# Last feed-forward stage of a two-block transformer step: three pairs of column chunks by seven block products instead of two, one weight sum of each on a DMA

## The reference

```python
h2 = rmsnorm_2(x, norm_mlp_g[l])
up = jnp.square(jax.nn.relu(jnp.einsum('bsd,df->bsf', h2, w_up[l])))   # w_up 1024 x 4096
x = x + jnp.einsum('bsf,fd->bsd', up, w_down[l])                       # w_down 4096 x 1024
```

## Time and profile before

| | us |
|---|---|
| median of 3 runs | 981.1 (980.86 to 981.48) |
| the profiled execution, its own time | 980.97 |
| its span, first to last instruction | 979.2 |
| TensorE busy | 970.4 (99%) |
| VectorE busy | 765.6 (78%) |
| ScalarE busy | 658.5 (67%) |
| GpSimd busy | 118.9 (12%) |

### The profile page before, as it was taken

The page is one execution under the profiler, slowest core; times in us unless marked ns, Lnnn a source line. Parts: engine busy times, 40 slices in busy tenths (PEclk is TensorE's granted clock), DMA queues, the critical chain, the costliest instruction groups (busy, mean ns, idle before and its releaser), DMA issues.

```text
span 979.2 us, 12257 instructions
## 1 busy us (share of the span) xinstructions
PE 970.4 (99%) x4528; PEld 796.2 (81%) x4528; DVE 765.6 (78%) x1010; ACT 658.5 (67%) x887; POOL 118.9 (12%) x109
## 2 busy tenths in 40 slices
PE   8999999999999999999999999999999999999998
PEld 7788888888777788888888788888888888888887
DVE  6798797668987666888797677777689878977675
ACT  7677576577666536766566586868875548877782
POOL 0000000022300000000000041159913001000000
DMA  8998937696444536986826586677666664695532
GB/s 263 314 313 276 278 117 234 198 322 193 134 152 146 172 129 215 274 254 212 267 67 224 167 249 227 168 177 204 205 214 215 234 196 151 211 319 170 191 111 94
DMA packets 167589, 202.12 MB, mean 206 GB/s; under 512 B 58081, under 2 KB 113770, under 8 KB 167402
## 3 DMA queue, kind: packets, MB, share of 16 engines
q1 hardware_dynamic: 166938, 201.21, 66.6%
q10 hardware_dynamic: 592, 0.14, 0.1%
HBM read 182.45 MB, written 5.77 MB: 192 GB/s over the span
## 4 chain that ended last, share of the span: by engine, by line
PE 92%; DVE 3%; DMA 2%; ACT 1%; issue 1%; POOL 1%; SPq 0%; ACTq 0%; DVEq 0%; POOLq 0%
PE bank L2650 22%; PE bank L2652 22%; PE bank L2651 22%; PE bank L2803 4%; PE bank L2805 4%; PE bank L2804 4%; PE bank L2923 3%; PE bank L2921 3%; PE bank L2922 3%; PE bank L2665 1%; DMA raw<-in_ffn_w_down 1%; PE bank L2957 1%; PE bank L3072 1%; DVE lo L1820 1%; DVE lo L1837 0%
## 5 line engine op out<-in xcount | busy, mean ns | idle before, releaser
L2650 PE MATMUL bank<-hi,xh 128*128 128x512 f32 (+1 forms) x824 | 328.0, 398 | 0.9 <-DVE lo L2251 0.7
L2652 PE MATMUL bank<-hi,xl 128*128 128x512 f32 (+1 forms) x824 | 320.6, 389 | 0.0
L2651 PE MATMUL bank<-lo,xh 128*128 128x512 f32 (+1 forms) x824 | 319.8, 388 | 0.0
L1820 DVE TENSOR_TENSOR lo<-raw,hi 128x2048 fp32r<-128x2048 f32 (+1 forms) x87 | 198.4, 2285 | 59.9 <-ACT hi L1114 59.7
L1114 ACT ACTIVATE hi<-raw 128x2048 fp32r<-128x2048 f32 (+1 forms) x90 | 170.8, 1902 | 86.9 <-PE bank L2652 37.1
L2650 PEld LDWEIGHTS bank<-hi,xh 128*128 128x128 f32 x824 | 154.8, 188 | 34.2 <-issue 1.7
L2652 PEld LDWEIGHTS bank<-hi,xl 128*128 128x128 f32 x824 | 154.7, 188 | 32.7
L2651 PEld LDWEIGHTS bank<-lo,xh 128*128 128x128 f32 x824 | 155.0, 188 | 29.8
L1837 DVE TENSOR_TENSOR lo<-raw,hi 128x1024 fp32r<-128x1024 f32 (+1 forms) x108 | 132.3, 1234 | 40.3 <-ACT hi L1123 39.5
L1123 ACT ACTIVATE hi<-raw 128x1024 fp32r<-128x1024 f32 x102 | 104.5, 1051 | 10.0 <-PE bank L2652 10.0
L2803 PE MATMUL bank<-hi,hh 128*128 128x512 f32 x176 | 69.2, 393 | 2.2 <-DVE hl L1946 2.2
(11 more groups left out here) (315 smaller groups left out, 1499.8 us busy)
## 6 DMA issues: line engine op xcount, KB each, us to landing
raw<-in_w_in SPq DMA_DIRECT2D x48, 1024.0 KB
raw<-in_ffn_w_gu SPq DMA_DIRECT2D x50, 512.0 KB
raw<-in_ffn_w_down SPq DMA_DIRECT2D x22, 1024.0 KB
first_operand<-in_ffn_w_gu SPq DMA_DIRECT2D x32, 512.0 KB
raw<-in_w_down SPq DMA_DIRECT2D x16, 1024.0 KB
raw<-in_w_out SPq DMA_DIRECT2D x8, 1024.0 KB
last_operand<-in_w_up SPq DMA_DIRECT2D x8, 1024.0 KB
raw<-in_w_up SPq DMA_DIRECT2D x8, 1024.0 KB
```

The source lines that it names most:

```text
L1820: nc.vector.tensor_tensor(lo[s][:, :, 0:width], whole(n)[:, :, 0:width], hi[s][:, :, 0:width].bitcast(F32), ALU.subtract).then_inc(lo_done, 1)
L2650: nc.tensor.matmul(o, sh, wh, start=first and j == 0, stop=False, skip_group_check=onto)
L2651: nc.tensor.matmul(o, sh, wl, start=False, stop=False, skip_group_check=onto)
L2652: ins = nc.tensor.matmul(o, sl, wh, start=False, stop=last and j == 3, skip_group_check=onto)
```

## The change

- `PAIRS = (2, 4, 6)`: chunks 4 and 5 become a pair, in the unit order of the other two; `plain_chunks` and `plain_up`'s waits for it go.
- In the last stage the fourth sum of each pair (operand 1 += operand 5) leaves VectorE and becomes a DMA with `accum_op=add` on GpSimd's queue, SBUF to SBUF, 1 MB. ScalarE's `split_hi` of p4 waits for it (`t4_in`), and so does the next pair's second sum, which overwrites operand 5. `SUMS_MADE` counts four sums per pair in the gated stages and three in the last.
- The other three sums of the next pair move into `pair_chunks` on VectorE: the first behind `add_product(j, 1)` and ahead of the split of p3, the second behind the split of p2 of the next pair and ahead of `last_lo(i)`, the third behind the split of p6.
- SyncE's order in the last stage is one loop over the pairs; the load of the next pair's block 3 now stands ahead of `flip_last(i, 1)`.
- Gated stages: `ffn_planes(f, i+1, ...)` moves ahead of `ffn_hi(f, i)` in `gated_pair`, and in the second pair `ffn_hi(f, 9)`, `ffn_merge(f, 9)` and `ffn_lo(f, 9)` move in front of, or between, the steps of chunk 10.

```diff
-PAIRS = (2, 6)
+PAIRS = (2, 4, 6)
...
@@ block_free
-                elif PAIR_AT[j][1] == PAIRS[1] or j in (1, 3):
+                elif j > LAST_PAIR:
+                    sp_eng.wait_ge(lo_done, pair_unit(j - 1, ("p1", "p4", "p7", "p3")[b]) + 1)
+                    if b == 0:
+                        sp_eng.wait_ge(pairs.t_made, SUMS_MADE[j - 1] + 1)
+                    elif b == 3:
+                        sp_eng.wait_ge(pairs.t_made, SUMS_MADE[j])
+                elif j in (1, 3):
...
@@ SyncE, last stage
+            for j in range(LAST_PAIR, len(PAIR_AT)):
+                i = PAIR_AT[j][1]
+                if i < NF2 - 2:
+                    last_block(j + 1, 0)
+                last_load("d", i - 1, 1)
+                last_load("d", i, 0)
+                flip_last(i, 0)
+                if i < NF2 - 2:
+                    last_block(j + 1, 2)
+                    last_block(j + 1, 1)
+                last_load("d", i, 1)
+                if i < NF2 - 2:
+                    last_block(j + 1, 3)
+                flip_last(i, 1)
+                last_load("d", i + 1, 0)
+                flip_last(i + 1, 1)
+                flip_last(i + 1, 0)
+            last_load("d", NF2 - 1, 1)
...
@@ GpSimd, at its end
+            def fourth_sum(j):
+
+                pool.wait_ge(pairs.t_made, SUMS_MADE[j] + 2)
+                pool.wait_ge(lo_done, pair_unit(j, "p2") + 1)
+                nc.gpsimd.dma_start(last_operand[1][:, :, :], last_operand[5][:, :, :],
+                                    accum_op=ALU.add).then_inc(pairs.t4_in, UNIT_IN)
...
@@ ScalarE gated_pair
+                ffn_planes(f, i + 1, 1)
+                ffn_planes(f, i + 1, 0)
                 ffn_hi(f, i)
                 split_hi(n + 12)
-                ffn_planes(f, i + 1, 1)
-                ffn_planes(f, i + 1, 0)
+                if j % 2 == 1:
+                    ffn_hi(f, i + 1)
                 ffn_act(f, i + 2, 0)
...
@@ VectorE gated_pair
                 split_lo(n + 12)
+                if j % 2 == 1:
+                    ffn_merge(f, i + 1)
                 ffn_hidden(f, i + 2, 0)
+                if j % 2 == 1:
+                    ffn_lo(f, i + 1)
                 ffn_hidden(f, i + 2, 1)
...
@@ VectorE pair_chunks, last stage (from the first pair's branch on)
-                    weight_sum(j, 4)
...
                     add_product(j, 0)
                     split_lo(unit_of("p6", i))
+                    weight_sum(j, 3)
                     split_lo(unit_of("d", i - 2, 1))
...
                 add_product(j, 1)
+                if more:
+                    weight_sum(j + 1, 1)
                 split_lo(unit_of("p3", i))
                 split_lo(unit_of("d", i - 1, 1))
                 last_merge(i)
                 add_product(j, 2)
                 split_lo(unit_of("d", i - 1, 1) + 1)
-                last_lo(i)
-                split_lo(unit_of("d", i - 1, 1) + 2)
+                if more:
+                    split_lo(unit_of("d", i - 1, 1) + 2)
+                    weight_sum(j + 1, 2)
+                    last_lo(i)
+                else:
+                    last_lo(i)
+                    split_lo(unit_of("d", i - 1, 1) + 2)
```

More of the change, by code:

```diff
@@ L128 @@
 LAST_PAIR = len(PAIR_AT) - len(PAIRS)
+SUMS_MADE = [4 * min(j, LAST_PAIR) + 3 * max(0, j - LAST_PAIR)
+             for j in range(len(PAIR_AT) + 1)]
 def unit_of(kind, i, b=0):
@@ L1107, in split_hi @@
                 elif KINDS[n] in OPERAND:
-                    act.wait_ge(pairs.t_made, 4 * pair_of(n) + {"p5": 1, "p6": 2, "p7": 3, "p4": 4}[KINDS[n]])
+                    j = pair_of(n)
+                    if KINDS[n] == "p4" and j >= LAST_PAIR:
+                        act.wait_ge(pairs.t4_in, UNIT_IN * (j - LAST_PAIR + 1))
+                    else:
+                        act.wait_ge(pairs.t_made, SUMS_MADE[j] + {"p5": 1, "p6": 2, "p7": 3, "p4": 4}[KINDS[n]])
                 else:
@@ L1449, in last_ffn @@
                 last_hi(0)
[L1450 to L1454, removed]
+                for j in range(LAST_PAIR, len(PAIR_AT)):
+                    pair_chunks(j)
                 split_hi(UNITS - 2)
@@ L1880, in weight_sum @@
                     dve.wait_ge(pairs.b_in[3], UNIT_IN * (j + 1))
+                    if j > LAST_PAIR:
+                        dve.wait_ge(pairs.t4_in, UNIT_IN * (j - LAST_PAIR))
                 elif t == 4:
@@ L1884, in weight_sum @@
                 if t > 1:
-                    dve.wait_ge(pairs.t_made, 4 * j + t - 1)
+                    dve.wait_ge(pairs.t_made, SUMS_MADE[j] + t - 1)
                 dst, left, right = ((4, 2, 0), (5, 3, 4), (2, 3, 2), (1, 1, 5))[t - 1]
@@ L2117, in pair_chunks @@
                 i = PAIR_AT[j][1]
+                more = j + 1 < len(PAIR_AT)
                 split_lo(unit_of("d", i - 2, 0))
@@ L2124, in pair_chunks @@
                     split_lo(unit_of("d", i - 2, 1))
-                    weight_sum(j, 4)
                     split_lo(unit_of("p7", i))
                     last_merge(i - 1)
+                    split_lo(unit_of("p5", i))
+                    last_lo(i - 1)
                 else:
@@ L2177, in last_ffn @@
                 sum_lo(2, 1)
-                for i in range(2, NF2, 2):
-                    if i in PAIRS:
-                        pair_chunks(PAIR_AT.index((2, i)))
-                    else:
-                        plain_chunks(i)
+                for j in range(LAST_PAIR, len(PAIR_AT)):
+                    pair_chunks(j)
                 split_lo(UNITS - 2)
@@ L2835, in plain_up @@
                     for t in range(NT):
-                        if i > 1 and u == 0 and i % 2 == 0:
-                            if t == 0:
-                                pe.wait_ge(last.acted, acted_before(i))
-                            else:
-                                pe.wait_ge(pairs.added, 3 * (LAST_PAIR + len([x for x in PAIRS if x < i])) - 2)
-                        elif i > 1 and u == 0 and t == 0:
-                            pe.wait_ge(pairs.added, 3 * (LAST_PAIR + len([x for x in PAIRS if x < i])))
                         ins = portion(n, t, (G, X)[i % 2][t], xh, xl, 4 * u, u == 0, u == 1)
@@ L2935, in last_ffn @@
                         last_down(i, b)
-                    elif kind != "u":
+                    else:
                         product(PAIR_AT.index((2, i)), kind)
-                    elif b == 0:
-                        plain_up(i)
             def warm(count):
```

66 lines of the change are left out of this document (4 added, 62 removed).

## The result

The changed kernel takes 998.58 us (median of four runs, 998.34 to 1002.09) against 981.15 (four runs of the kernel before, 980.86 to 981.48): a ratio of 1.0185, interval 1.0172 to 1.0198. It is **17.4 us slower**, where 11.8 were forecast, and 0.6 us above the upper end of the range. In the changed kernel `split_hi` is L1123, `split_lo` L1810, `weight_sum` L1879, the copy into planes L1359, `last_merge` L2090, the transposes L735, and the loads of blocks L717.

A forecast was written before the change was run, and what follows sets the result against it. TensorE, busy 970.4 of 979.2 us, was taken as the bound: 980.97 - 2.7 (matmuls) - 2.5 (gated waits) + 8.6 + 8.5 (handovers) = 992.9, stated as 992.8 us; range 983.0 to 998.0, some 8 in 10.

The forecast's parts named there:

- the transpose of chunk 2: SyncE, first handover: issued at 861.7 behind block 3's load, lands at 867.7 (864.8 to 868.7), making p1 3.1 us late.
- 12 matmuls: Last stage, chunks 4 and 5: seven products of 12 replace 96 matmuls by 84, all on the path, -2.7 us.
- waits at d(9): Gated stages: earlier planes and transposes of chunk 9 remove both TensorE waits, -2.5 us (between -2.5 and 0).
- handover 2 to 4: p1, p2, d: First three units of pair 4 start late by 3.1, 2.6 and 2.9 us, together 8.6, none coming back.
- handover 4 to 6: p1, p2, d: The pattern repeats at pair 6: 3.05, 2.6 and 2.9 us late, together 8.5.
- half clock: TensorE falling to 1.2 GHz after handover waits: nothing in the forecast sum.
- rival F: Handover waits also cost clock: one 24-matmul unit at 1.2 GHz per handover, twice 2.7 us, about 998; 5%.
- B: Handovers cost only their minimum: block 3's load and the transpose overlap, so the transpose is not later; 983.6; 15%.
- the floor: Each handover costs at least 3.9 us if the transpose comes no later: d(2,0) starts at 879.4 instead of 875.54.
- C: Adding DMA exceeds its 20 us, each us over costing one in every pair; at 25 us, 1007.9; 6%.
- D: Faster: p2 and d(2,0) met within 2.6 us in each handover; with none lost, 975.8; 7%.
- E: One handover is covered and the other costs its minimum: 979.7, no change to be measured; 5%.

The follow-up runs named there:

- 978.84: Changed kernel with chunk i's transpose ahead of block 3's load and ScalarE's split of p2 ahead of `last_hi` and `square 3`: 978.84 us, ratio 0.9982.
- 978.56: Changed kernel with transpose ahead of block 3's load, p2's split ahead of `last_hi` and `square 3`, `last_lo` ahead of the second sum: 978.56 us, ratio 0.9966.
- 977.57: Changed kernel with transpose, p2's split and `last_lo` moved ahead, and chunk 9's gated transposes ahead of the weight load: 977.57 us, ratio 0.9961.
- 983.33: Changed kernel with transpose and p2's split moved ahead, and the second sum behind the next pair's d(i,0) split: 983.33 us, ratio 1.0025.
- 991.77: Changed kernel with only ScalarE's split of p2 moved ahead of `last_hi` and `square 3`: 991.77 us, ratio 1.0102.

## Why the prediction went wrong, point by point

The direction, the places and the order of the causes were right: six waits, on `lo`, at the first three units of pairs 4 and 6, with the transpose of chunk 2 as the first cause and ScalarE's planes waiting for it. The time was 5.8 us too low. In the last stage it is by the sizes of terms; the step on the gated stages was wrong in kind. Measured is the profiled execution:

| term | forecast | measured |
|---|---|---|
| 12 matmuls | -2.7 | -2.72 |
| waits at d(9) | -2.5 | -1.0 |
| handover 2 to 4: p1, p2, d | 3.1 + 2.6 + 2.9 | 4.05 + 2.63 + 2.89 |
| handover 4 to 6: p1, p2, d | 3.05 + 2.6 + 2.9 | 3.85 + 2.63 + 2.89 |
| half clock | 0 | 1.6 |
| start of this execution | 0 | 0.8 |

**The transpose of chunk 2** was to land at 867.7, with bounds of 864.9 and 868.7. It landed at 868.4 in an execution that was 0.3 us ahead of the one before, so it is the upper bound, 868.7. The walk from there on was right to 0.03 us a unit. The failing step was the time that DMAs take in SyncE's queue, and it failed twice. The load of block 2 was to take 5.9 to 7.0 us and land by 856.5; it took 7.9 and landed at 856.85, so that the sum, p3's `lo`, the load of block 3 and the transpose all came 0.6 to 0.8 us later than forecast, with the 0.3 us counted in. In the kernel before the same load had taken 7.3 us (849.52 to 856.82): the 5.9 of the earlier trace rows was another load's. Then the transpose was priced with "5.6 for this one and 1 us more", 6.0 us from its own issue; it took 6.4, and 7.0 in the second handover, where a maximum of 7.0 stood in the earlier trace rows for a transpose issued 1.3 us behind a load. Taken as the value and not as the end of the range, that row would have met the first landing, in part by luck, since the late load would have made up for what was too much. Together p1 is 0.95 and 0.8 us later than forecast, 1.8 in all.

**The gated waits** fell by the same error. The transposes were to land "3 to 4 us later"; I had moved their issue and not asked what stands ahead of them in the queue. The first took 6.8 us. This is the step that was wrong in kind; the run with the transposes ahead of the load shows it. 1.5 us.

**The clock.** In the sum it was nothing, and the rival at 5% put it at 5.4 us. It fell in each handover, and cost 1.6 us in all in this execution, since the slow matmuls of p1 ran while p2's `lo` was being made; only those in the `d` units were on the path. The four executions have mean clocks of 0.991 to 0.995, the slowest (1002.09 us) the lowest, so this price differs from one to the next. So rival F's mechanism was there, at a third of its price; that its total came near the result (998) is chance.

**The other rivals.** B (983.6) wanted a transpose that does not become later: it is the run with the transpose first, 986.39, which lost 3.9 us in the first handover, as the floor says, and 3.05 in the second, and some clock. C is out: the DMA took 7.9 us at most, and landed 9 to 12 us before p4's split began. D's condition, at most 2.6 us a handover, is met by the two moved steps, with 978.84 and 978.56. E did not occur.

**The range** ended at 998.0, with the handovers at their bound of 9.6 each making 995. With the gated gain at zero instead of -2.5 the same sum is 997.5, and the clock would have come on top: the upper bounds of three terms were never added up together, though two of them hang on one unknown, how long a transpose takes behind a load.

## What to carry to other kernels

When an issue is moved, look at its whole queue: here a small transfer issued behind a large one landed about 1 us after it, and when engines wait for it in line it can delay each unit behind it. Where a row exists for the like case, take it as the value and not as the bound, and read a transfer's time off that very transfer where the trace has it. And before a step is moved ahead of or behind another, price also what is queued behind the engine that waits for it: in the sum moved behind the split of d(2,0), that was the larger part.

## What the runs showed of the hardware

**A transpose behind a load.** On SyncE's queue the transpose of the handover took 3.8 us in the kernel before and 4.0 with the transpose first, ahead of a 1 MB load, and 6.4 and 6.8 us when issued 0.5 us behind one; in the gated stages 6.8 us behind three. Of all 192 transposes of the last stage in the twelve traces, the eight that were issued 0.5 us behind a load took 6.3 to 7.0 us, and those issued more than 6 us behind one 2.8 in the median. Moving one transpose ahead is not free for the next: in the run with the transpose first the two that follow the moved ones took 7.6 and 8.2 us, where the changed kernel has 2.8, and no unit waited for them. In the four of the changed kernel and of the run with the first sum later, the load landed first and the transpose 1.0 to 1.2 us after it. The Trainium skill (DMA: Bandwidth & Descriptors, Queues, rings and completion order) says that each DMA engine consumes the descriptors of a ring in order, though a later one may finish its write first; by that rule the transpose's descriptors start behind the load's, and these rows agree.

**The clock after waits.** In the changed kernel TensorE was granted 1.2 instead of 2.4 GHz from 874.0 to 877.4, 884.3 to 887.7 and 925.2 to 928.6. Waits of 3.89, 2.60 and 3.69 us ended there. It did not fall at each such wait: d(4,0) waited 2.59 us and its row stands at full clock. With the fourth sum back on VectorE the same d(4,0) waited 2.58, and there it fell. In the kernel before and in the four changed ones with waits of at most 1.4 us in the stage (977.57, 978.84, 978.56 and 983.33 us) it stayed at 1.000. The Trainium skill (TensorE: Matmul & The Clock Gate, HAM oscillation) tells of a kernel whose bursts of matmuls between waits for data each start at the low clock. The rows agree for some waits and not for all; a price for every wait would have been too high here also because a slow unit costs only where nothing is waited for behind it.

**The adding DMA.** 1 MB from SBUF to SBUF with an addition took 7.7 to 7.9 us from issue to landing in the changed kernel. In the four kernels in which ScalarE's split of p2 goes first (978.56, 991.77, 978.84 and 977.57 us) the one of pair 4 took 9.8 to 12.3 us, and the other two 7.7 to 8.1; in the fifth such kernel (983.33 us) none took more than 8.2. The estimate of twice a load, 12 us, was its upper end. Whether other transfers or the merges on VectorE stretch it was not taken apart.
